# Layer norm of a Hawk/Conformer step: sums on GpSimd, eight square buffers, centring first, gates and variance between projection blocks

## What is computed

```python
proj = hm @ w_in + b_in                                  # 1024 -> 6 x 1024
u_lru, gate_lru, conf_a, conf_b, bg_lru, bg_conf = split(proj)
xc = causal_dwconv(u_lru, width 4)
r = sigmoid(xc @ wa + ba); i = sigmoid(xc @ wx + bx)     # 16 blocks of 64 x 64
a = exp(-8 * r * softplus(-lam)); h = scan(a, sqrt(1 - a*a) * i * xc)
out_a = (h * gelu(gate_lru)) @ w_lru_o
dc = causal_dwconv(conf_a * sigmoid(conf_b), width 31)
mu = mean(dc); var = mean((dc - mu)**2)                  # over the 1024 channels
out_b = silu((dc - mu) * rsqrt(var + eps) * g + b) @ w_conf_o
merged = sigmoid(bg_lru) * out_a + sigmoid(bg_conf) * out_b
x = x + gt1 * (merged @ w_out)                           # then a mixture of 16 experts
```

## Time and profile before

| what | value |
|---|---|
| median of 3 runs | 1026.93 us (1023.51 to 1027.47) |
| the profiled execution's own time | 1024.94 us |
| its span, first to last instruction | 1023.2 us |
| mean granted TensorE clock | 0.941 |
| PE busy | 881.3 us (86%) |
| DVE busy | 722.2 us (71%) |
| ACT busy | 434.9 us (43%) |
| POOL busy | 240.7 us (24%) |

### The profile page before, as it was taken

One profiled execution on the slowest core, in us unless ns is written; L12 is line 12 of the kernel. 1 busy time (PEld: TensorE's weight loads), 2 busy tenths in 40 slices (PEclk: granted clock), 3 DMA queues, 4 the chain that ended last, 5 costly groups with the idle time before them and its releaser, 6 DMA issues. The chain is left out here.

```text
span 1023.2 us, 12585 instructions
## 1 busy us (share of the span) xinstructions
PE 881.3 (86%) x5140; PEld 718.7 (70%) x5140; DVE 722.2 (71%) x945; ACT 434.9 (43%) x409; POOL 240.7 (24%) x175
## 2 busy tenths in 40 slices
PE   2559999999998998999999995499799999999920
PEld 1158787899996987899995453378587777777710
DVE  2370699999995888854112564689987898887828
ACT  0552332333326505123210122077477776776613
POOL 3031635445540011033330231201011111120030
PEclk9769999999999999999999997599899999999965
DMA  8984746342220013033446104379699999999743
GB/s 281 296 292 154 244 147 227 124 129 84 83 93 32 1 44 121 8 131 124 139 175 249 42 21 190 128 259 360 231 366 385 363 342 380 365 348 368 283 175 111
DMA packets 79413, 201.93 MB, mean 197 GB/s; under 512 B 6956, under 2 KB 39852, under 8 KB 71128
## 3 DMA queue, kind: packets, MB, share of 16 engines
q1 hardware_dynamic: 72875, 181.58, 49.9%
q0 software_dynamic: 6480, 19.54, 5.0%
HBM read 187.44 MB, written 18.44 MB: 201 GB/s over the span
## 5 line engine op out<-in xcount | busy, mean ns | idle before, releaser
L734 POOL TENSOR_TENSOR w_lo<-ring_a,w_hi 128x2048 fp32r<-128x2048 f32 x28 | 129.0, 4607 | 336.0 <-ACT w_hi L896 336.0
L1786 DVE TENSOR_TENSOR slot_c<-ring_a,slot_c 128x2048 fp32r<-128x2048 f32 x72 | 164.0, 2288 | 31.6 <-ACT slot_c L1052 31.2
L1267 PE MATMUL ps<-hm_hi,w_hi 128*128 128x272 f32 x768 | 161.4, 291 | 0.1
L1052 ACT ACTIVATE slot_c<-ring_a 128x2048 fp32r<-128x2048 f32 x72 | 137.9, 1917 | 50.4 <-DMA ring_a<-in_w_down 36.3
L1267 PE MATMUL ps<-hm_hi,w_lo 128*128 128x272 f32 x768 | 158.3, 288 | 0.0
L1267 PE MATMUL ps<-hm_lo,w_hi 128*128 128x272 f32 x768 | 158.2, 288 | 0.0
L1630 DVE SCALAR_TENSOR_TENSOR ps<-region_b,rt,ps 128x512 f32<-128x512 f32 x208 | 137.7, 750 | 0.0
L1267 PEld LDWEIGHTS ps<-hm_hi,w_hi 128*128 128x128 f32 x768 | 120.0, 189 | 14.3 <-issue 12.1
L1425 PE MATMUL ps<-slot_c,xgt_hi 128*128 128x512 f32 x384 | 125.5, 398 | 2.6 <-issue 2.6
L1267 PEld LDWEIGHTS ps<-hm_lo,w_hi 128*128 128x128 f32 x768 | 120.5, 189 | 0.0
L1267 PEld LDWEIGHTS ps<-hm_hi,w_lo 128*128 128x128 f32 x768 | 120.0, 189 | 0.0
(11 more groups left out here) (325 smaller groups left out, 1378.5 us busy)
## 6 DMA issues: line engine op xcount, KB each, us to landing
ring_a<-in_w_gate SPq DMA_DIRECT2D x32, 1024.0 KB, 8.3
ring_a<-in_w_up SPq DMA_DIRECT2D x32, 1024.0 KB, 7.2
ring_a<-in_w_down SPq DMA_DIRECT2D x32, 1024.0 KB, 7.0
ring_a<-in_w_in SPq DMA_DIRECT2D x24, 1024.0 KB, 6.7
region_c<-in_w_ada SPq DMA_DIRECT2D x16, 1024.0 KB, 7.1
y_scr<-region_d POOLq DMA_DIRECT2D x16, 512.0 KB, 7.2
ring_a<-in_w_ada SPq DMA_DIRECT2D x3, 2048.0 KB, 18.8
y_scr<-region_e SPq DMA_DIRECT2D x1, 4096.0 KB, 17.4
```

Source lines behind the costliest of these rows:

```text
L734: g.tensor_tensor(w_lo[:, q % 2], raw[split_at[q] % 2], w_hi[:, q % 2].bitcast(F32), ALU.subtract)\
L1052: s_.activation(hi_slot(n), raw_slot(n), ACT.Copy).then_inc(unit_hi, 1)
L1267: ins = mm(ps[:, 2 * (n % 2) + h, 0:HALF], w[:, q % 2, k, m * P:(m + 1) * P], x[:, k, h * HALF:(h + 1) * HALF], start=(k == 0 and w is w_h ...
L1786: v.tensor_tensor(lo_slot(n), raw_slot(n), hi_slot(n).bitcast(F32), ALU.subtract).then_inc(unit_lo, 1)
```

## The change

`add_block` lets POOL add up the eight blocks of `dc` as they are finished, so that `mean` is two matmuls on the sum. Centring is two instructions of four blocks each and stands ahead of the four `lru_conv` on DVE. The squares have eight buffers and no handshake with PE. In `work`, `var` stands after the second block of `G_BC`, the gates of the first group after the second and third block; those of the second group after the fourth block of the second `G_BC` half and after the first `co` block there. The multiplication by the reciprocal root is eight instructions, the silu waits for each, and each of the eight steps of a `co` block waits for its own block of silu; `lo` waits for the halves of `z_lo`. The reciprocal in `lru_1` is two halves, `gated` of a `co` block between them; `lru_2` and what follows move behind more of the `gated`. The silu and the tanh stand around the drain of the fourth `G_BC` block.

```diff
+        ln_sq = carve(region_b, 4352, (KC, T))
+        dc_sum = carve(region_d, 6528 + 2 * T, (T,))
...
             if g == G_GATE + 1:
                 work += [("mean", 0, 0)]
-                work += [(x, 0, m) for m in range(GC) for x in ("r", "i")]
-                work += [("var", 0, 0)]
         for h, w in ((0, "co"), (1, "co"), (0, "lo"), (1, "lo")):
             g = (G_BC if w == "co" else G_BL) + h
             for m in range(GC):
                 work += [("in", g, m)]
-                if (h, w, m) == (1, "co", 1):
-                    work += [(x, 1, c) for c in range(GC) for x in ("r", "i")]
-            work += [(w, h, m) for m in range(GC)]
+                if (h, w, m) == (0, "co", 1):
+                    work += [("var", 0, 0)]
+                    work += [(x, 0, c) for c in range(2) for x in ("r", "i")]
+                if (h, w, m) == (0, "co", 2):
+                    work += [(x, 0, c) for c in range(2, GC) for x in ("r", "i")]
+                if (h, w, m) == (1, "co", GC - 1):
+                    work += [(x, 1, c) for c in range(2) for x in ("r", "i")]
+            for m in range(GC):
+                work += [(w, h, m)]
+                if (h, w, m) == (1, "co", 0):
+                    work += [(x, 1, c) for c in range(2, GC) for x in ("r", "i")]
...
+            def add_block(k):
+                pool.wait_ge(dc_ok, k + 1)
+                if k > 1:
+                    pool.wait_ge(dc_summed, k - 1)
+                g.tensor_tensor(dc_sum, dc[:, 0, :] if k == 1 else dc_sum, dc[:, k, :], ALU.add).then_inc(dc_summed, 1)
...
             products(7)
+            add_block(6)
+            add_block(KC - 1)
             for q in range(16, len(split_at)):
                 split_lo(q)
...
             def squares():
-                act.wait_ge(cent_ok, 1)
+                act.wait_ge(last_tr, 1)
                 for k in range(KC):
-                    if k >= 2:
-                        act.wait_ge(sq_used, k - 1)
-                    s_.activation(ln_sq[:, k % 2, :], dc[:, k, :], ACT.Square).then_inc(sq_ok, 1)
+                    act.wait_ge(cent_ok, k // GC + 1)
+                    s_.activation(ln_sq[:, k, :], dc[:, k, :], ACT.Square).then_inc(sq_ok, 1)
...
-                if (kind, g, m) == ("var", 0, 0):
+                if (kind, g, m) == ("in", G_BC, 0):
                     squares()
...
             def chunk(n, w, m, rhs):
                 for k in range(KC):
+                    pe.wait_ge(sn_ok, k + 1)
...
             def chunk_split(n, q, m, x_hi, x_lo):
                 for k in range(KC):
+                    if x_hi is z_hi and k % GC == 0:
+                        pe.wait_ge(z_lo_ok, k // GC + 1)
...
-                    pe.wait_ge(dc_ok, KC)
-                    for k in range(KC):
-                        for h in range(2):
-                            ins = mm(ps[:, 2 * (n % 2) + h, 0:HALF], ones[:, :], dc[:, k, h * HALF:(h + 1) * HALF],
-                                     start=(k == 0), stop=(k == KC - 1))
+                    pe.wait_ge(dc_summed, KC - 1)
+                    for h in range(2):
+                        ins = mm(ps[:, 2 * (n % 2) + h, 0:HALF], ones[:, :], dc_sum[:, h * HALF:(h + 1) * HALF],
+                                 start=True, stop=True)
...
+            for h in range(2):
+                hs = slice(h * GC, (h + 1) * GC)
+                v.tensor_tensor(dc[:, hs], dc[:, hs], ln_mean.unsqueeze(1).to_broadcast([P, GC, T]), ALU.subtract)\
+                 .then_inc(cent_ok, 1)
+            last_rows(0, 62, 0)
             dve.wait_ge(ada_sum, 12)
             for k in range(GC):
                 lru_conv(k)
...
-            v.tensor_tensor(dc, dc, ln_rstd.unsqueeze(1).to_broadcast([P, KC, T]), ALU.mult).then_inc(ln_ok, 1)
+            for k in range(KC):
+                v.tensor_tensor(dc[:, k, :], dc[:, k, :], ln_rstd, ALU.mult).then_inc(ln_ok, 1)
...
             lru_1(0)
             gated("co", 0, 0)
+            lru_1b(0)
+            gated("co", 0, 1)
+            gated("co", 0, 2)
             lru_2(0)
-            gated("co", 0, 1)
+            gated("co", 0, 3)
             lru_3(0)
-            gated("co", 0, 2)
             lru_4(0)
-            gated("co", 0, 3)
```

More of the change, by code:

```diff
@@ L146, in build @@
         ln_rstd = carve(region_d, 6528 + T, (T,))
-        ln_sq = carve(region_d, 6528 + 2 * T, (2, T))
+        ln_sq = carve(region_b, 4352, (KC, T))
+        dc_sum = carve(region_d, 6528 + 2 * T, (T,))
         tt = carve(region_b, 4352, (GC, T))
@@ L334, in build @@
         sq_ok = sem("sq_ok")
-        sq_used = sem("sq_used")
         ln_ok = sem("ln_ok")
+        dc_summed = sem("dc_summed")
         sn_ok = sem("sn_ok")
@@ L781, in _ @@
             products(4)
+            for k in range(1, 4):
+                add_block(k)
             split_lo(10)
@@ L784, in _ @@
             products(5)
+            add_block(4)
             split_lo(12)
@@ L787, in _ @@
             products(6)
+            add_block(5)
             split_lo(14)
@@ L993, in _ @@
                         split_hi(q)
-                    if work[n] == ("co", 1, 0):
-                        root(1)
+                    if work[n] in (("co", 0, 2), ("co", 1, 2)):
+                        root(work[n][1])
                     continue
@@ L1000, in _ @@
                     act.wait_ge(mod_store, 16)
-                if (kind, g, m) == ("var", 0, 0):
+                if (kind, g, m) == ("in", G_BC, 0):
                     squares()
-                if (kind, g, m) == ("in", G_BC, 2):
-                    act.wait_ge(ln_ok, 1)
+                if (kind, g, m) == ("in", G_BC, 3):
                     for k in range(KC):
+                        act.wait_ge(ln_ok, k + 1)
                         s_.activation(dc[:, k, :], dc[:, k, :], ACT.Silu, bias=rt[:, k, R_LNB:R_LNB + 1],
@@ L1032, in _ @@
                         s_.activation(z_hi[:, hs], z[:, hs], ACT.Copy).then_inc(z_hi_ok, 1)
-                if kind == "i" and m == GC - 1:
+                if (kind, g, m) in (("in", G_BC, GC - 1), ("i", 1, GC - 1)):
+                    g = int(kind == "i")
                     act.wait_ge(sp_ok, 1)
@@ L1040, in _ @@
                     ins.then_inc(t_ok, 1)
-                if (kind, g, m) == ("in", G_BC, GC - 1):
-                    root(0)
             def unit_high(n):
@@ L1284, in _ @@
                         pe.wait_ge(raw_full[f % 2], 16 * (f // 2 + 1))
[L1285 to L1288, removed]
                     drained(pe, n - 2)
@@ L1317, in _ @@
                         for h in range(2):
-                            ins = mm(ps[:, 2 * (n % 2) + h, 0:HALF], ones[:, :], ln_sq[:, k % 2, h * HALF:(h + 1) * HALF],
+                            ins = mm(ps[:, 2 * (n % 2) + h, 0:HALF], ones[:, :], ln_sq[:, k, h * HALF:(h + 1) * HALF],
                                      start=(k == 0), stop=(k == KC - 1))
-                        if k < KC - 1:
-                            ins.then_inc(sq_used, 1)
                     ins.then_inc(pairs, 1)
@@ L1668, in lru_1, with lru_1b @@
                 ch.link(v.tensor_scalar(rec, tt, 1.0, None, ALU.add))
-                v.reciprocal(rec, rec).then_inc(t_copied, 1)
+                ch.link(v.reciprocal(rec[:, 0:2], rec[:, 0:2]))
+            def lru_1b(g):
+                v.reciprocal(rec[:, 2:GC], rec[:, 2:GC]).then_inc(t_copied, 1)
                 dve.wait_ge(t_copied, g + 1)
@@ L1714, in _ @@
                 conformer(k)
+            n = place[("mean", 0, 0)]
+            dve.wait_ge(pair_act, sum(by_act[:n + 1]))
+            for h in range(2):
[3 more added lines that the diff above has]
+            last_rows(0, 62, 0)
             dve.wait_ge(ada_sum, 12)
@@ L1718, in _ @@
                 lru_conv(k)
[L1720 to L1723, removed]
             n = place[("var", 0, 0)]
@@ L1757, in _ @@
             last_rows(1, 35, 1)
+            gated("co", 1, 0)
             lru_1(1)
-            gated("co", 1, 0)
+            gated("co", 1, 1)
+            lru_1b(1)
+            gated("co", 1, 2)
+            gated("co", 1, 3)
             lru_2(1)
-            gated("co", 1, 1)
             lru_3(1)
-            gated("co", 1, 2)
             lru_4(1)
-            gated("co", 1, 3)
             for h in range(2):
```

## The result

The changed kernel takes 1018.72 us (median of 20 runs), the kernel before in the same runs 1023.93 (20 runs, 1017.97 to 1029.72). The ratio is 0.9946, 95% interval 0.9928 to 0.9964: 5.5 us less, by the interval 3.7 to 7.4. One of the 20 runs of the changed kernel took 1332.44 us at a mean granted clock of 0.646 and is not in the ratio. The changed kernel is faster by a little over 0.5%, and 1018.7 lies in the range of 1007 to 1020; but the sum had promised 12.9 less, and the 1013 stood on a median of 1026.93 for three runs of the kernel before, which over 20 runs is 3.0 lower. The profiled execution of the changed kernel took 1018.70 (span 1016.7); PE is busy for 877.5 us, DVE 716.8, ACT 433.3, POOL 249.2, the mean granted clock is 0.941. The two profiles differ also where nothing was changed: the first projection block starts at 71.4 us before and 67.9 after.

A forecast was written before the change was run, and what follows sets the result against it. The PE queue was taken to set the pace in the mixer. Terms -6.4 - 6.1 + 3.0 - 1.0 + 1.5 - 4.1 + 0.2 = -12.9 took the profiled 1024.94 to 1012.0; forecast median 1013 us, range 1007 to 1020.

The forecast's parts named there:

- Mean: Mean on PE: four records in place of 32, 0.9 for 7.3, 6.4 us less; POOL's seven adds cost nothing.
- the worst case: POOL's seventh add for the mean ends at 294.3, the low part behind it at 298.9, with 0.3 to spare.
- The hold of the centring: DVE's centring is held until POOL's low part ends at 304.8; the opposing no-hold rival gave 1010, chance 0.15.
- the term of +3.0: New PE pause of 3.0 us ahead of the variance, released by ACT's drain; bounds 0 and 4.2.
- Variance: Variance on PE: 32 records no longer wait for squares, 7.3 instead of 9.2, 1.9 us less.
- First gates, `co`, second gates: PE's gates and first `co` half: first gates 1.0 less, `co` 1.5 more, second gates 4.1 less.
- After it: `lru_2` to `lru_4` of the second group move behind the last `co` drain: cost nothing, uncovered up to some 3 us.
- the waits inside `co` and `lo` blocks: Rival: new PE waits there break overlap of weight loads and matmuls; 0.2 each, 16 us, 1029; chance 0.07.
- Given back: Rival: transfers set what follows the mixer; if experts' loads are bound to a fixed time, half lost, 1020; chance 0.06.
- The second sign of being wrong: The first `G_BL` block begins near 434 and the end of the kernel does not move with it.
- the clock rival: Rival: PE's clock falls behind the new pause ahead of the variance, 1.9 us more, 1015; chance 0.22.
- late bounds ahead of the first `G_BL` block: Late bounds of the chains, added as 1 + 3 to the 1015 for the slow end of the range.

The follow-up runs named there:

- Experiment 4: Changed kernel, but POOL waits for both centring halves before its low part of the piece for `G_BC` blocks 2 and 3; 1012.67 us, ratio 0.9881.
- Experiment 5: Changed kernel, but the mean is again 32 matmuls of PE over the eight blocks and POOL adds nothing; 1019.86 us, ratio 0.9966.
- experiment 1: Changed kernel, but the second group's four scans read one of their two inputs from PSUM, order unchanged; 1013.3 us, ratio 0.9881.
- experiment 2: Changed kernel, but all eight second-group gate products stand ahead of its first `co` block, `lru_2` to `lru_4` between the gated products; 1017.66 us, ratio 0.9929.
- the eighth kernel: Changed kernel plus scans reading PSUM, POOL's low part waiting for the centring, and a first-group gated product between the two half reciprocals; 1006.76 us, ratio 0.9838.
- experiment 3: Changed kernel, but ACT makes the high half of z's second half behind the drain of the fourth `G_BL` block, not the second; 1020.56 us, ratio 0.9948.

## Why the prediction was right in its range and wrong in its size

- **Mean**: 7.50 to 1.08 us of records, 0.9 by starts, as forecast; the adds cost PE nothing. POOL's last add ran from 287.41 to 288.77, ahead of where the worst case had it.
- **The hold of the centring**: right, and the term of +3.0 measured 2.52. Experiment 4 shows its cause: without the hold there is no pause. POOL started 0.47 us ahead of DVE, where the sum had 0.6. Experiment 5 shows what the sum did not say: the pause belongs to the mean's price. Of 6.4 us the early mean was worth 3.75 until the low part was moved.
- **Variance**: 7.60 for 9.45, without a fall of the clock in the changed kernel's profiles. The rival that the clock falls behind the new pause came true in experiments 1 and 2, with the same pause: 1.7 us, where 1.9 was priced. The Trainium skill (TensorE: Matmul & The Clock Gate, section Why this matters for your kernels) advises against idle gaps between bursts of matmuls, but it has longer gaps in mind than this one. Behind the pause of 2.52 to 2.53 the trace agrees with it in two profiles, 9.29 us, and not in three, 7.60.
- **First gates, `co`, second gates**: mean to first `co` block 10.25 less (forecast 10.5), the `co` half 1.81 more (1.5 forecast, of which 1.2 at the third block and 0.3 at the fourth; 1.29 of idle time is seen ahead of the third, and the fourth starts at 362.87, right behind the drain that ends at 362.76), from there to the first `G_BL` block 3.76 less (3.9).
- **The step that failed** is "After it": the move of `lru_2` to `lru_4` behind the last `co` drain was costed at nothing, "covered" by 24 us of four blocks, without the cover up to some 3 us. It cost 5.2. The cover would have been long enough: experiment 1 has the same order and no wait ahead of `lo`. What was missing in the sum were POOL's two low parts, 7.7 and 14.9 us behind the first `G_BL` block in the kernel before (454.72 and 461.92 against 446.98), into whose time the chain was moved. The sum had used the hold for the centring, from a 128x32 product that ended with POOL's, and did not ask it of the scans. 8.7 us of hold on the scans then passed down: DVE to ACT's `z_hi`, that to ACT's drains, those to PE, which waits 2.65 and loses 1.6 by the clock behind it; the other 0.90 is for the most part POOL's low part, stretched by the first scan from 4.6 to 5.32. The 20.3 us that the sum took for this chain already contain one such hold, of some 3.8 us, on the second group's first 128x32 product, which the sum did not see. DVE and POOL of the kernel before:

```profile
440.69 3.95 DVE L1693 TENSOR_TENSOR region_d<-region_b,rt 128x32 f32<-128x32 f32 x1
440.05 4.52 POOL L734 TENSOR_TENSOR w_lo<-ring_a,w_hi 128x2048 fp32r<-128x2048 f32 x1 [45.84 <-ACT w_hi L896]
```

- **The rivals**: the waits inside `co` and `lo` blocks cost nothing that shows: 29.50 us for four `co` blocks in the eighth kernel, 29.49 before, and 72.97 for the stretch of the `lo` blocks in both. "Given back" came out near in time (1020), by another mechanism than the one named: the loss that was found lies in the mixer. The second sign of being wrong came half true: the first `G_BL` block came 12.2 us earlier by the stretches, and the end moved by 5.5.
- **The range** held 1018.7 partly by luck. Its slow end was made of the clock rival and of late bounds ahead of the first `G_BL` block, and none of that is where the time went. With the median of 20 runs in place of that of three, the same sum would have given 1010 and a range that ends at 1017.

The Trainium skill (SBUF — State Buffer, section Who interferes with whom) says that a DVE instruction with two SBUF inputs contends with a GpSimd instruction that reads SBUF, and that the order of issue decides who is blocked. The trace agrees on both: 5.55 us for a scan issued behind POOL's low part, 5.32 instead of 4.6 for a low part issued 0.30 us behind a scan, and 4.55 for four scans with one input in PSUM.

## What to carry to other kernels

Work that is moved must be laid beside what the other engines do where it arrives: list what GpSimd runs there, and ask of each moved VectorE instruction whether all its operands lie in SBUF; cover counts only if what lies under it runs at its own speed. A step made earlier is worth only what the next step can take, so look at what that step now overlaps before the saving is booked. A hold can be cheap to lift: here one wait on GpSimd and one operand in PSUM gave back 7.6 us.

## What the runs showed of the hardware that was not expected

- A scan of 128x512 is held like a product: 5.55 and 5.58 us for 1.20. With one input in PSUM four of them took 4.55 beside POOL, as long as without POOL (4.57).
- Not only instructions with two inputs are held: a 128x32 copy inside SBUF took 3.63 us beside POOL's low part in experiment 4, and 0.16 without it in the changed kernel.
- The clock falls behind a pause of about 2.5 us in some executions and not in others of the same work. Behind 2.52 to 2.53 ahead of the variance it fell in experiments 1 and 2 (variance 9.29 us) and not in the change's two profiles or in experiment 3 (7.60). Behind 2.65 ahead of `lo` it fell in the change's two profiles and not in experiments 4 and 5 (first `lo` block 6.08 and 6.07 instead of 7.62 and 7.48). It fell also behind 2.63 ahead of `G_BL` in experiment 2 and behind 2.38 ahead of `lo` in experiment 3, and not behind the 2.54 in the middle of that block. It costs 1.4 to 1.7 us each time; a sum can hold it only as a chance.
- The start of the first projection block has two places in the twelve profiles, 66.9 to 67.9 and 71.4 to 71.7 us, in kernels that are alike up to there.
